# Weight tiles 512 bytes longer, with each unit's chunks at one of sixteen byte offsets, and a halved dynamic DMA scratch

## The chip, the cores and the metric

The kernel runs on one core of one Trainium2 chip. The metric is the device time of one execution in microseconds. A profiled execution gives the trace from which all rows below are taken.

## What is computed

Three layers of a transformer on 512 tokens (x) and 256 context tokens (ctx), width 2048, all in fp32. Cut to what matters for the weights:

```python
# layer 1, attention:  w_in is 2048 x 5120, w_out is 2048 x 2048
h = rmsnorm(x, pre_g) * (1 + scale) + shift ; hc = the same of ctx
proj = h @ w_in ; kv_c = hc @ w_in[:, 2048:3072]
y = concat(dense_attention, window_attention) * silu(z)
x = x + gate * rmsnorm(y @ w_out, post_g)
# layer 2, pooling: w_in is 2048 x 4096
proj = h @ w_in
y = (pooled(proj[:, :2048]) @ pool_w) * pool_scale * silu(proj[:, 2048:])
x = x + gate * rmsnorm(y @ w_out, post_g)
# layer 3: w_in is 2048 x 8192
proj = h @ w_in_2
y = concat(stick_breaking(q, k, v) * silu(z), group_norm(retention(q, k, v)) * silu(z))
x = x + gate * (y @ w_out_2)
# shift, scale, gate of each layer: silu(c) @ (2048 x 6144) + b
```

## The kernel before

**Chunks.** Every weight matrix is cut into units of 256 output columns (a few of 512, or of several column blocks side by side), and every unit into chunks of 512 KB: four slices of 128 rows by 256 columns, so 4 KB in each of the 128 partitions. There are 88 units and 376 chunks, numbered in one line through the three layers. Chunk i passes through four steps. SyncE loads it with one DMA into RAW[i % 5] (L1135) once TensorE is done with chunk i - 5. ScalarE rounds it to fp32r into the tile that `whi(i)` names (L1357, recorded at its helper L1272) once TensorE is done with chunk i - 4: WHI0, WHI1, WHI2 for i % 4 below 3, and WHITA for i % 4 = 3, or WHIY in the middle of layer 3. VectorE writes the rest, RAW - WHI, over RAW as WLO (L1751, recorded at L1634). TensorE then multiplies: each slice and each half of its columns takes three matmuls, the high part of the weights with the high and the low part of the activations (HHI, HLO) and the low part of the weights with HHI. That makes 4 x 2 x 3 = 24 matmuls of 512 columns a chunk.

**Roles.** All matmuls are recorded at the helper's line L2151 and all transposes at L2154. The trace names a matmul as out<-moving,stationary: `G<-HHI,WLO` streams 512 columns of HHI over a loaded 128 x 128 block of WLO. In `mm` and `mm2` stages the weights are the stationary operand. In `mt` (values of layer 1, 256 columns wide) and `mw` (values of layer 3, 512 columns wide) the weights are the moving operand: `G<-WLO,HHI`.

**Order.** The order on all engines is one list, written out by `make_plan`, which every engine's program walks. Side work (normalisation, rope, scores, softmax, the modulation vectors, whose weights stream through MWIDE) is put between the matmuls of the chunks.

**Places.** Tiles are laid out by hand in SBUF. The first free byte of a partition is 16,481, which rounds to 16,512, that is 128 above a multiple of 512. All large tiles up to MK are multiples of 512 bytes long, so HHI, HLO, RAW, WHI0 to WHI2, WHIY, MWIDE, SQ, TY and the like all start at 128 modulo 512. The small vectors behind them are not such multiples, so that the scratch region (base `s0`) starts at 384 modulo 512, and with it WHITA, PHI, PLO, QLO, KLO, PB, PT and XR. No tile that a matmul of 128 or more columns reads starts off a multiple of 64 bytes. HHI lies at 16,512, WHIY at 110,720, WHI0 at 135,296, WHITA at 224,128, PHI at 203,136 bytes.

```python
        tile, at = place(f"RAW{i}", [P, 4, 256], F32)
        WLO.append(place(f"WLO{i}", [P, 4, 256], F32R, at)[0])
    WHI3 = [place(f"WHI{i}", [P, 4, 256], F32R)[0] for i in range(3)]
...
                if i >= NR:
                    e.wait_ge(p_gemm, i - NR)
                e.o.dma_start(shaped(RAW[i % NR], chunks[i].shape[1]), chunks[i])
...
                cp(whi(i)[:, :, :], RAW[i % NR][:, :, :])
...
                tt(WLO[i % NR][:, :, :], RAW[i % NR][:, :, :], f(whi(i)[:, :, :]), SUB)
```

Of the kernel before, what the change touches and what calls it, by code (L numbers as in the profile page):

```python
# [5 lines left out]
F32 = mybir.dt.float32  # L6
F32R = mybir.dt.float32r
# [4 lines left out]
P = 128  # L12
D = 2048
KT = 16
SEQ = 512
# [64 lines left out]
def build(nc, ctx, T, out):  # L80
# [4 lines left out]
    top = [(base + 63) // 64 * 64]  # L85

    def place(name, shape, dt, at=None):
        size = 4
        for s in shape[1:]:
            size *= s  # L90
        if at is None:
            at = top[0]
            top[0] += (size + 31) // 32 * 32
            assert top[0] <= end - 32, (name, top[0], end)
        return nc.alloc_sbuf_tensor_at(name, list(shape), dt, offset=at), at

    HHI, h0 = place("HHI", [P, KT, SEQ], F32R)
    HLO, _ = place("HLO", [P, KT, SEQ], F32R)
    Y, y0 = place("Y", [P, KT, SEQ], F32)
    CT, _ = place("CT", [P, KT, CTX], F32, y0)  # L100
    CLO, _ = place("CLO", [P, KT, CTX], F32R, y0)
    CHI, _ = place("CHI", [P, KT, CTX], F32R, y0 + 4 * KT * CTX)
    XN = [place(f"XN{i}", [P, D], F32, h0 + 4 * i * D)[0] for i in range(6)]
    LATE = [place(f"LATE{i}", [P, 4, 256], F32, h0 + 4 * SEQ * (KT + 8 + 2 * i))[0] for i in range(4)]
    NR, NS = 5, 4
    RAW, WLO = [], []
    for i in range(NR):
        tile, at = place(f"RAW{i}", [P, 4, 256], F32)
        RAW.append(tile)
        WLO.append(place(f"WLO{i}", [P, 4, 256], F32R, at)[0])  # L110
    WHI3 = [place(f"WHI{i}", [P, 4, 256], F32R)[0] for i in range(3)]
    MRAW, MWIDE = [], []
    for i in range(2):
        tile, at = place(f"MRAW{i}", [P, 4, 256], F32)
        MRAW.append(tile)
        MWIDE.append(place(f"MWIDE{i}", [P, 2, 512], F32, at)[0])
    MACC, _ = place("MACC", [P, 512], F32)
    d0 = top[0]
    SQ2 = [place("SQ0", [P, SEQ], F32)[0]]
    tile, sq1 = place("SQ1", [P, SEQ], F32)  # L120
# [3 lines left out]
    QHI, _ = place("QHI", [P, SEQ], F32R, ty0)  # L124
    TT_, _ = place("TT", [P, SEQ], F32)
    DUMP, _ = place("DUMP", [P, D], F32, d0)
    RB, _ = place("RB", [P, 6, P], F32, d0 - 2048)
    IDN, _ = place("IDN", [P, P], F32)
    ONE, _ = place("ONE", [P, P], F32)
    CS, _ = place("CS", [P, SEQ], F32)  # L130
    SN, _ = place("SN", [P, SEQ], F32)
    MK, mk0 = place("MK", [P, 3, P], F32)
    COL, _ = place("COL", [P, 304], F32)
    MOD, _ = place("MOD", [P, 3, 48], F32)
    MODX, _ = place("MODX", [P, 32], F32)
    SC, _ = place("SC", [P, 48], F32)
    SM, _ = place("SM", [P, 48], F32)
    s0 = top[0]
    room = end - 32 - s0

    def scratch(name, shape, dt, off):
        size = 4
        for s in shape[1:]:
            size *= s
        assert off + size <= room, (name, off, size, room)
        return place(name, shape, dt, s0 + off)[0]

    K1 = 1024
# [26 lines left out]
    LSB = scratch("LSB", [P, SEQ], F32, 40 * K1)  # L175
    WB = [scratch(f"WB{i}", [P, SEQ], F32, 42 * K1 + i * 2 * K1) for i in range(2)]
    TA = [scratch(f"TA{i}", [P, SEQ], F32, 46 * K1 + i * 2 * K1) for i in range(2)]
    WHI_TA = scratch("WHITA", [P, 4, 256], F32R, 46 * K1)
    WHI_Y, _ = place("WHIY", [P, 4, 256], F32R, y0 + 4 * SEQ * 14)
    TRIR = scratch("TRIR", [P, P], F32R, 50 * K1)  # L180
    RESTR = scratch("RESTR", [P, P], F32R, 50 * K1 + 512)
    XO = [scratch(f"XO{i}", [P, SEQ], F32, 32 * K1 + i * 2 * K1) for i in range(4)]
    KLO = scratch("KLO", [P, 4, 768], F32R, 0)
    KHI = [place(f"KHI{i}", [P, 768], F32R, y0 + at)[0] for i, at in enumerate((16 * K1, 19 * K1, 24 * K1))]
# [4 lines left out]
    SQLO, _ = place("SQLO", [P, SEQ], F32R, sq1)  # L189
    SQHI, _ = place("SQHI", [P, SEQ], F32R, tm0)  # L190
    ONER, _ = place("ONER", [P, P], F32R, mk0)
# [18 lines left out]
    raw = [sig(f"raw{i}") for i in range(NR)]  # L210
# [8 lines left out]
    def on_chip(*names):  # L219
# [7 lines left out]
    a_intro, a_whi, a_xt, a_sq, a_rs, a_row, a_h, a_ev, a_exp, a_turn, a_silu, a_sqy = on_chip(  # L227
        "a_intro", "a_whi", "a_xt", "a_sq", "a_rs", "a_row", "a_h", "a_ev", "a_exp", "a_turn", "a_silu", "a_sqy")
    a_ph, a_st, a_out, a_sum = on_chip("a_ph", "a_st", "a_out", "a_sum")
    v_intro, v_wlo, v_xt, v_rs, v_xn, v_cols, v_h, v_acc, v_msum, v_mod, v_nr, v_sm, v_gate, v_silu = on_chip(  # L230
        "v_intro", "v_wlo", "v_xt", "v_rs", "v_xn", "v_cols", "v_h", "v_acc", "v_msum", "v_mod", "v_nr", "v_sm", "v_gate",
        "v_silu")
# [5 lines left out]
    MUL, ADD, SUB, MAX, MIN = ALU.mult, ALU.add, ALU.subtract, ALU.max, ALU.min  # L238

    def f(t):  # L240
        return t.bitcast(F32)
# [8 lines left out]
    def shaped(tile, nk):  # L250

        return tile[:, :, :].rearrange("p a n -> p (a n)").rearrange("p (t n) -> p t n", t=nk)
# [19 lines left out]
    units = [both(ev_w, 2048, 2304), weight(ev_w, 2560), weight(ev_w, 2816)]  # L272
# [28 lines left out]
    chunks = [c for u in units for c in u]  # L301
# [4 lines left out]
    stick0, stick1 = first_chunk[third + 1], first_chunk[third + 15] + 4  # L306
# [3 lines left out]
    last_y = max(i for i in fourths if i < stick1)  # L310
    next_ta = min(i for i in fourths if i >= stick1)

    def whi(i):

        if i % 4 < 3:
            return WHI3[i % 4]
        return WHI_Y if stick0 <= i < stick1 else WHI_TA

    nat = [("c", 0), ("c", 1)] + [("x", i) for i in range(4)]
    order0 = [nb for i in range(8) for nb in (i, 8 + i)]  # L320
# [794 lines left out]
    def sp_program(e):  # L1115
        e.o.dma_start(PR[:, :, :], T["small"].rearrange("a p n -> p a n")).then_inc(*par.up("par", by=16))
        e.o.dma_start(IDN[:, :], T["t_sq"][0]).then_inc(*cst.up("idn", by=16))
        e.o.dma_start(ONE[:, :], T["t_sq"][1]).then_inc(*cst.up("cst", by=16))
        for n in range(6):
            src = T["ctx"][0, n * P:(n + 1) * P, :] if n < 2 else T["x"][0, (n - 2) * P:(n - 1) * P, :]  # L1120
            e.o.dma_start(XN[n][:, :], src).then_inc(*xnd[n].up(n, by=16))
        for stage, *a in plan:
            if stage == "job_load":
                i, = a
                slot = job_slot[i]
                if job_before[i] is not None:
                    e.wait_ge(p_row, job_before[i])
                nb, c = jobs0[i]
                e.o.dma_start(rings[slot][:, :, :], weight(T["ev_mod_w"][0], 256 * nb)[c]).then_inc(  # L1129
                    *mraw[slot].up(("job", i), by=16))  # L1130
            elif stage == "load":
                i, = a
                if i >= NR:
                    e.wait_ge(p_gemm, i - NR)
                e.o.dma_start(shaped(RAW[i % NR], chunks[i].shape[1]), chunks[i]).then_inc(*raw[i % NR].up(i, by=16))  # L1135
            elif stage == "mod_load":
                n, = a
                if n >= 2:
                    e.wait_ge(v_acc, n - 2)
                else:  # L1140
                    e.wait_ge(p_row, last_in[n])
                w, nb, _, _, _ = mod_jobs[n // 8]
                e.o.dma_start(MWIDE[n % 2][:, :, :], wide(w, nb, n % 8)).then_inc(*mraw[n % 2].up(n, by=16))
            elif stage == "x_out":
                q, i = a
                if q == 3:
                    if i % 2:
                        e.wait_ge(v_out, (q, i))
                    else:
                        e.wait_ge(a_out, (q, i))  # L1150
                    e.o.dma_start(out[0, i * P:(i + 1) * P, 512 * q:512 * q + 512], XO[i][:, :]).then_inc(
                        *last[i].up((q, i), by=16))
        for i in range(4):
            e.wait_ge(last[i], (3, i))
# [108 lines left out]
    def act_program(e):  # L1263
# [7 lines left out]
        def cp(o, i, scale=1.0):  # L1271
            return e.o.activation(o, i, ACT.Copy, scale=scale)  # L1272
# [29 lines left out]
        for stage, *a in plan:  # L1302
            if stage == "x_sum":
                n, = a
# [21 lines left out]
            elif stage == "row_copy":  # L1326
                n, = a
# [17 lines left out]
            elif stage == "split":  # L1345
# [7 lines left out]
                elif i == next_ta:  # L1353
                    e.wait_ge(p_cum, (7, 0))
                    e.wait_ge(v_st, (7, 0, "ls"))
                    e.wait_ge(v_st, (7, 0, "lo"))
                cp(whi(i)[:, :, :], RAW[i % NR][:, :, :]).then_inc(*a_whi.up(i))  # L1357
            elif stage == "k_copy":
                side, nt, pair, u = a
                kh = 2 * side + nt  # L1360
# [268 lines left out]
    def dve_program(e):  # L1629
# [3 lines left out]
        def tt(o, a, b, op):  # L1633
            return e.o.tensor_tensor(o, a, b, op)  # L1634
# [43 lines left out]
        for stage, *a in plan:  # L1678
# [69 lines left out]
            elif stage == "split":  # L1748
                i, = a
                e.wait_ge(a_whi, i)  # L1750
                tt(WLO[i % NR][:, :, :], RAW[i % NR][:, :, :], f(whi(i)[:, :, :]), SUB).then_inc(*v_wlo.up(i))  # L1751
            elif stage == "mod_acc":
                t, c = a
                n = 8 * t + c
# [390 lines left out]
    def pe_program(e):  # L2145
# [35 lines left out]
        for stage, *a in plan:  # L2181
# [45 lines left out]
            elif stage == "kv":  # L2227
                k, what, part = a
                i = k // 4 * 2 + (0 if what == "k" else 1)
                wh, wl, j = whi(i), WLO[i % NR], k % 4  # L2230
                hi, lo = HHI[:, k, :], HLO[:, k, :]
                chi, clo = CHI[:, k, :], CLO[:, k, :]
                begin, end = k == 0, k == KT - 1
# [23 lines left out]
                    t.then_inc(*p_gemm.up(i, *([(0, 1 if what == "k" else "v")] if end else [])))  # L2257
            elif stage == "mm":
                kind, layer, u, i, c, nt, jj, pair, last = a
                wh, wl = whi(i), WLO[i % NR]  # L2260
                cols = slice(nt * P, nt * P + P)
                e.wait_ge(v_wlo, i)
                for j in (2 * jj, 2 * jj + 1):
# [16 lines left out]
                        t.then_inc(*p_gemm.up(*named))  # L2280
            elif stage == "mm2":
                kind, layer, u, i, uu, k0, nt, jj, pair = a
                wh, wl = whi(i), WLO[i % NR]
                cols = slice(nt * P, nt * P + P)
                e.wait_ge(v_wlo, i)
                for j in (2 * jj, 2 * jj + 1):
# [15 lines left out]
                                              *([(u, nt)] if k == 15 and uu == 2 else [])))  # L2302
            elif stage == "mt":
                layer, u, i, c, t_, pair, last, final = a
                wh, wl = whi(i), WLO[i % NR]
                bank = (G[pair] + [OB])[t_ // 2]
                o = bank[:, t_ % 2 * 256:t_ % 2 * 256 + 256]
                e.wait_ge(v_wlo, i)
# [18 lines left out]
                    t.then_inc(*p_gemm.up(i, *([(u, 1)] if last else [])))  # L2327
            elif stage == "mw":
                layer, u, i, c, t_, pair, last, final = a
                wh, wl = shaped(whi(i), 2), shaped(WLO[i % NR], 2)  # L2330
                o, cols = G[pair][t_ % 2][:, :], slice(t_ * P, t_ * P + P)
                e.wait_ge(v_wlo, i)
                for j in range(2):
# [300 lines left out]
```

## Time and profile before

| | us |
|---|---|
| median of 2 runs | 2536.39 (2535.85 to 2536.93) |
| the profiled execution's own time | 2535.82 |
| its span in the trace | 2534.0 |
| TensorE busy | 2497.7 (99%) |
| TensorE weight loads | 2020.2 (80%) |
| VectorE busy | 1623.8 (64%) |
| ScalarE busy | 973.6 (38%) |
| GpSimd busy | 110.7 (4%) |

The profiled execution took 1.8 us more than its span and 0.6 us less than the median of the runs. The granted TensorE clock was 0.995 over the span. A matmul's record runs until its last result is out (some 389 ns for 512 columns), and the next one begins before that; what counts for throughput is the distance between starts, which the chain of work shows as length over count.

### The profile page before, as it was taken

To read this page: it belongs to the slowest core of one execution; us is meant where nothing else is said; L and a number is where in the kernel's file an instruction comes from. 1 tells how busy PE (TensorE), PEld (TensorE's weight loads), DVE (VectorE), ACT (ScalarE), POOL (GpSimd) and SP (SyncE) were. 2 spreads that over 40 slices of the span, in tenths; PEclk is the share of its full clock that TensorE was granted. 3 is DMA by queue.
4 is the path that set the end of the run, shared out by engine and by line. 5 is a ranking of instruction groups with operands and counts; after the bars stand their busy time and mean duration, and the time that the engine had idled before them with its cause. 6 is when DMAs were issued, how large, how long until landed. Compare 5 with 4: busy or idle time off the path is not lost.

```text
span 2534.0 us, 30108 instructions
## 1 busy us (share of the span) xinstructions
PE 2497.7 (99%) x11975; PEld 2020.2 (80%) x11975; DVE 1623.8 (64%) x2444; ACT 973.6 (38%) x1549; POOL 110.7 (4%) x117
## 2 busy tenths in 40 slices
PE   7999999999999999999999999999999999999999
PEld 4789777777777887888888887888888787887887
DVE  4456776677776768776776768456365577656532
ACT  4232444444444333432434333445455432333421
POOL 0000000000000114000000113000000000000000
PEclk8999999999999999999999999999999999999999
DMA  9955433434433754666645754323222245532342
GB/s 350 336 193 185 127 110 121 125 125 133 132 101 136 258 180 157 208 200 211 200 162 175 249 175 158 111 76 91 80 87 84 75 151 169 175 112 89 123 154 83
DMA packets 293133, 390.58 MB, mean 154 GB/s; under 512 B 11698, under 2 KB 221234, under 8 KB 289154
## 3 DMA queue, kind: packets, MB, share of 16 engines
q1 hardware_dynamic: 287184, 355.84, 43.5%
q0 software_dynamic: 5808, 32.84, 3.5%
q8 instruction: 94, 1.54, 0.2%
q14 instruction: 45, 0.37, 0.1%
q10 hardware_dynamic: 2, 0.00, 0.0%
HBM read 371.85 MB, written 16.78 MB: 153 GB/s over the span
## 4 chain that ended last, share of the span: by engine, by line
PE 89%; DVE 5%; DMA 2%; ACT 2%; issue 1%; SPq 1%; POOL 0%; DVEq 0%; ACTq 0%; POOLq 0%
PE G L2151 74%; PE OB L2151 6%; PE S L2151 6%; PE TB L2154 2%; PE TB L2151 1%; DMA MRAW<-in_ev_mod_w 1%; DMA MORE<-in_ev_mod_w 1%; DVE WLO L1634 1%; DVE MACC L1640 1%; DVE TT L1634 1%; ACT PB L1445 1%; DVE SM L1862 0%; SPq L1129 0%; PE OB L2154 0%; DVE Y L1634 0%
## 5 line engine op out<-in xcount | busy, mean ns | idle before, releaser
L2151 PE MATMUL G<-HHI,WLO 128*128 128x512 f32 x2560 | 1001.0, 391 | 0.0
L2151 PE MATMUL G<-HHI,WHI 128*128 128x512 f32 x1964 | 801.8, 411 | 0.5 <-DVE CLO L1640 0.5
L2151 PE MATMUL G<-HLO,WHI 128*128 128x512 f32 x1928 | 753.2, 391 | 1.6 <-DVE HLO L1640 1.4
L2151 PEld LDWEIGHTS G<-HHI,WLO 128*128 128x128 f32 x2560 | 480.7, 188 | 104.3
L1272 ACT ACTIVATE WHI<-RAW 128x1024 fp32r<-128x1024 f32 x282 | 297.5, 1056 | 560.9 <-PE G L2151 501.6
L1634 DVE TENSOR_TENSOR WLO<-RAW,WHI 128x1024 fp32r<-128x1024 f32 x282 | 344.5, 1222 | 234.9 <-ACT WHI L1272 233.0
L2151 PEld LDWEIGHTS G<-HHI,WHI 128*128 128x128 f32 x1964 | 370.9, 189 | 80.3 <-issue 6.7
L2151 PEld LDWEIGHTS G<-HLO,WHI 128*128 128x128 f32 x1928 | 363.1, 188 | 79.7 <-issue 6.7
L1640 DVE SCALAR_TENSOR_TENSOR MACC<-MWIDE,SC,MACC 128x512 f32<-128x512 f32 x420 | 320.4, 763 | 39.2 <-DMA MWIDE<-in_w_ada 12.8
L2151 PE MATMUL G<-HHI,WHITA 128*128 128x512 f32 x536 | 215.0, 401 | 0.0
L2151 PE MATMUL G<-HLO,WHITA 128*128 128x512 f32 x536 | 209.2, 390 | 0.0
L1634 DVE TENSOR_TENSOR WLO<-RAW,WHITA 128x1024 fp32r<-128x1024 f32 x76 | 93.1, 1226 | 91.4 <-ACT WHITA L1272 91.4
L2151 PE MATMUL G<-WLO,HHI 128*128 128x512 f32 (+1 forms) x384 | 136.1, 354 | 0.0
L2151 PEld LDWEIGHTS G<-HLO,WHITA 128*128 128x128 f32 x536 | 100.9, 188 | 19.9 <-DVE HLO L1640 0.8
L2151 PEld LDWEIGHTS G<-HHI,WHITA 128*128 128x128 f32 x536 | 100.8, 188 | 19.9 <-issue 0.5
L2151 PE MATMUL G<-WHI,HHI 128*128 128x512 f32 (+1 forms) x272 | 103.6, 381 | 0.6 <-ACT K L1272 0.6
L1272 ACT ACTIVATE WHITA<-RAW 128x1024 fp32r<-128x1024 f32 x76 | 80.3, 1056 | 58.2 <-PE G L2151 52.6
L1269 ACT ACTIVATE SQ<-SQ 128x512 f32<-128x512 f32 x144 | 90.6, 629 | 25.4 <-DVE SQ L1640 22.4
L2151 PE MATMUL G<-WHI,HLO 128*128 128x512 f32 (+1 forms) x272 | 97.5, 358 | 0.0
L2151 PEld LDWEIGHTS G<-WLO,HHI 128*128 128x128 f32 x384 | 72.5, 189 | 10.3
L2151 PE MATMUL OB<-PT,VV 128*128 128x512 f32 (+2 forms) x192 | 74.7, 539 | 0.0
L1445 ACT ACTIVATE PB<-S,SM,COL 128x768 f32<-128x768 f32 x32 | 31.7, 992 | 103.5 <-DVE SM L1637 103.5
(347 smaller groups left out, 3060.7 us busy)
## 6 DMA issues: line engine op xcount, KB each, us to landing
RAW<-in_w_in SPq DMA_DIRECT2D x128, 512.0 KB, 3.7
MWIDE<-in_od_mod_w SPq DMA_DIRECT2D x96, 512.0 KB, 4.1
MWIDE<-in_w_ada SPq DMA_DIRECT2D x96, 512.0 KB, 4.6
RAW<-in_ev_w_in SPq DMA_DIRECT2D x80, 512.0 KB, 3.5
RAW<-in_od_w_in SPq DMA_DIRECT2D x64, 512.0 KB, 3.9
MWIDE<-in_ev_mod_w SPq DMA_DIRECT2D x32, 512.0 KB, 3.8
RAW<-in_ev_w_out SPq DMA_DIRECT2D x32, 512.0 KB, 3.3
RAW<-in_od_w_out SPq DMA_DIRECT2D x32, 512.0 KB, 3.3
```

Source lines behind the costliest of these rows:

```text
L1269: return e.o.activation(o, i, fn, bias=bias, scale=scale)
L1272: return e.o.activation(o, i, ACT.Copy, scale=scale)
L1445: e.o.activation(PB[n % 2][:, lo:768], S[:, lo:768], ACT.Exp, bias=nm, scale=1.0 if banded(h) else q_root_of(h, qt), accum_out=SM[:, i + 1 ...
L1634: return e.o.tensor_tensor(o, a, b, op)
L1640: return e.o.scalar_tensor_tensor(out=o, in0=a, scalar=s, in1=b, op0=op0, op1=op1)
L2151: return e.o.matmul(o, l, r, start=start, stop=stop, skip_group_check=True)
L2154: return e.o.transpose(o, i, IDN[:, :])
```

## The change

RAW, WLO, WHI0 to WHI2 and WHITA grow from 1024 to 1152 floats a partition. A new function `inside` picks 1024 of them, starting at float `FROM[unit % 16]`: byte offsets 0, 32, 64, 96, 128, 16, 48, 80, 112, 160, 192, 256, 320, 384, 448 and 8 for units 0 to 15, then again from 0. All chunks of a unit lie at the same offset in all their tiles. From `stick0` to `stick1` (chunks 228 to 299, layer 3) the offset is 0 in all tiles, and WHIY has no more room than before. To make room, the scratch for DMAs whose descriptors GpSimd writes is set to 8192 bytes, where it was 16,384; the first free byte of a partition goes from 16,481 to 8,289, and everything lies lower. `s0` is rounded so that the scratch region starts at 128 modulo 512 as all else does; TRIR and RESTR move up by 512 bytes.

Of the 376 chunks, 100 stay at offset 0. Offsets that are multiples of 64 bytes have 117 chunks (20, 17, 21, 13, 20, 16, 10 at 64, 128, 192, 256, 320, 384, 448), offsets 32, 96 and 160 have 24, 24 and 16, offsets 16, 48, 80 and 112 have 17, 20, 32 and 16, and offset 8 has 10. That is 276 chunks off zero, of which 159 are off a multiple of 64 bytes and 95 off a multiple of 32.

The instructions of all engines, their shapes, their waits and their order are the same before and after; only addresses differ.

```diff
@@ -105,10 +105,10 @@
     for i in range(NR):
-        tile, at = place(f"RAW{i}", [P, 4, 256], F32)
+        tile, at = place(f"RAW{i}", [P, 1152], F32)
         RAW.append(tile)
-        WLO.append(place(f"WLO{i}", [P, 4, 256], F32R, at)[0])
-    WHI3 = [place(f"WHI{i}", [P, 4, 256], F32R)[0] for i in range(3)]
+        WLO.append(place(f"WLO{i}", [P, 1152], F32R, at)[0])
+    WHI3 = [place(f"WHI{i}", [P, 1152], F32R)[0] for i in range(3)]
@@ -135,6 +135,7 @@
+    top[0] += (128 - top[0]) % 512
     s0 = top[0]
@@ -175,10 +176,10 @@
-    WHI_TA = scratch("WHITA", [P, 4, 256], F32R, 46 * K1)
-    WHI_Y, _ = place("WHIY", [P, 4, 256], F32R, y0 + 4 * SEQ * 14)
-    TRIR = scratch("TRIR", [P, P], F32R, 50 * K1)
-    RESTR = scratch("RESTR", [P, P], F32R, 50 * K1 + 512)
+    WHI_TA = scratch("WHITA", [P, 1152], F32R, 46 * K1)
+    WHI_Y, _ = place("WHIY", [P, 1024], F32R, y0 + 4 * SEQ * 14)
+    TRIR = scratch("TRIR", [P, P], F32R, 50 * K1 + 512)
+    RESTR = scratch("RESTR", [P, P], F32R, 51 * K1)
@@ -310,11 +311,25 @@
+    unit_of = [u for u, n in enumerate(units) for _ in n]
+    FROM = (0, 8, 16, 24, 32, 4, 12, 20, 28, 40, 48, 64, 80, 96, 112, 2)
+
+    def inside(slot, i):
+
+        at = 0 if stick0 <= i < stick1 else FROM[unit_of[i] % 16]
+        return slot[:, at:at + 1024].rearrange("p (a n) -> p a n", a=4)
+
     def whi(i):
 
         if i % 4 < 3:
-            return WHI3[i % 4]
-        return WHI_Y if stick0 <= i < stick1 else WHI_TA
+            return inside(WHI3[i % 4], i)
+        return inside(WHI_Y if stick0 <= i < stick1 else WHI_TA, i)
+
+    def raw_of(i):
+        return inside(RAW[i % NR], i)
+
+    def wlo(i):
+        return inside(WLO[i % NR], i)
@@ -1132,7 +1147,7 @@
-                e.o.dma_start(shaped(RAW[i % NR], chunks[i].shape[1]), chunks[i]).then_inc(*raw[i % NR].up(i, by=16))
+                e.o.dma_start(shaped(raw_of(i), chunks[i].shape[1]), chunks[i]).then_inc(*raw[i % NR].up(i, by=16))
@@ -1354,7 +1369,7 @@
-                cp(whi(i)[:, :, :], RAW[i % NR][:, :, :]).then_inc(*a_whi.up(i))
+                cp(whi(i)[:, :, :], raw_of(i)[:, :, :]).then_inc(*a_whi.up(i))
@@ -1748,7 +1763,7 @@
-                tt(WLO[i % NR][:, :, :], RAW[i % NR][:, :, :], f(whi(i)[:, :, :]), SUB).then_inc(*v_wlo.up(i))
+                tt(wlo(i)[:, :, :], raw_of(i)[:, :, :], f(whi(i)[:, :, :]), SUB).then_inc(*v_wlo.up(i))
@@ -2257,7 +2272,7 @@
-                wh, wl = whi(i), WLO[i % NR]
+                wh, wl = whi(i), wlo(i)
...
@@ -2614,7 +2629,7 @@
-    nc = bacc.Bacc("TRN2", target_bir_lowering=False, num_devices=1)
+    nc = bacc.Bacc("TRN2", target_bir_lowering=False, num_devices=1, dynamic_dma_scratch_size=8192)
```

## Rows read from the trace of the kernel before

**Rows 1.** The page, parts 1 and 2: busy us (share), instructions; busy tenths by slice

```profile
PE 2497.7 (99%) x11975; PEld 2020.2 (80%) x11975; DVE 1623.8 (64%) x2444; ACT 973.6 (38%) x1549; POOL 110.7 (4%) x117
...
PE   7999999999999999999999999999999999999999
```

**Rows 2.** The chain that ended last, in pieces: start us, us, what

```profile
1473.47 43.56 PE G L2151 x192
...
2199.50 38.08 PE G L2151 x168
...
1005.77 10.88 PE G L2151 x48
...
189.56 5.75 PE G L2151 x48
...
346.90 1.04 PE S L2151 x6
347.94 1.41 PE G L2151 x6
349.34 0.43 PE TB L2154 x4
349.78 1.38 PE G L2151 x6
```

**Rows 3.** Timeline of PE across a change from WHI2 to WHITA: start us, us, instruction

```profile
2209.31 0.39 PE L2151 MATMUL G<-WLO,HHI 128*128 128x512 f32 x1
2209.53 0.39 PE L2151 MATMUL G<-WHI,HHI 128*128 128x512 f32 x1
2209.76 0.39 PE L2151 MATMUL G<-WHI,HLO 128*128 128x512 f32 x1
2209.99 0.39 PE L2151 MATMUL G<-WLO,HHI 128*128 128x512 f32 x1
2210.22 0.39 PE L2151 MATMUL G<-WHITA,HHI 128*128 128x512 f32 x1
2210.44 0.39 PE L2151 MATMUL G<-WHITA,HLO 128*128 128x512 f32 x1
2210.67 0.39 PE L2151 MATMUL G<-WLO,HHI 128*128 128x512 f32 x1
2210.89 0.39 PE L2151 MATMUL G<-WHITA,HHI 128*128 128x512 f32 x1
```

**Rows 4.** Groups of PE by shape, 1475 to 1515 us: busy us, mean ns

```profile
L2151 PE MATMUL G<-HHI,WHI 128*128 128x512 f32 x42 | 16.3, 389 | 0.0
L2151 PE MATMUL G<-HHI,WHITA 128*128 128x512 f32 x18 | 7.0, 389 | 0.0
```

**Rows 5.** Weight loads, timeline and group: 256-column matmuls, then 1475 to 1515 us

```profile
471.37 0.28 PE L2151 MATMUL S<-KHI,QHI 128*128 128x256 f32 x1
471.49 0.28 PE L2151 MATMUL S<-KLO,QHI 128*128 128x256 f32 x1
471.60 0.51 PE L2151 MATMUL S<-KHI,QLO 128*128 128x512 f32 x2
...
L2151 PEld LDWEIGHTS G<-HHI,WLO 128*128 128x128 f32 x59 | 11.1, 188 | 2.3
```

**Rows 6.** Groups of the page, part 5: busy us, mean ns, idle before, releaser

```profile
L1272 ACT ACTIVATE WHI<-RAW 128x1024 fp32r<-128x1024 f32 x282 | 297.5, 1056 | 560.9 <-PE G L2151 501.6
L1634 DVE TENSOR_TENSOR WLO<-RAW,WHI 128x1024 fp32r<-128x1024 f32 x282 | 344.5, 1222 | 234.9 <-ACT WHI L1272 233.0
```

**Rows 7.** Timeline of SP, ACT and DVE around chunk work, and PE 16 us later

```profile
2206.47 0.47 SPq L1135 DMA_DIRECT2D RAW<-in_w_in  x1
...
2211.43 1.06 ACT L1272 ACTIVATE WHI<-RAW 128x1024 fp32r<-128x1024 f32 x1 [5.33 <-DMA RAW<-in_w_in]
...
2212.52 1.22 DVE L1634 TENSOR_TENSOR WLO<-RAW,WHI 128x1024 fp32r<-128x1024 f32 x1 [0.86 <-ACT WHI L1272]
...
2226.53 0.39 PE L2151 MATMUL G<-WHI,HHI 128*128 128x512 f32 x1
```

**Rows 8.** DMA issues: KB each, us to landing; then one stretch, PE to DMA share, GB/s

```profile
RAW<-in_od_w_in SPq DMA_DIRECT2D x64, 512.0 KB, 3.9
...
XR<-x_spill POOLq DMA_DIRECT2D x12, 1024.0 KB, 6.2
...
1386.70:1428.00 41.30, 41.30 (x184) 34.21 (x183) 32.07 (x40) 17.05 (x25) 8.06 (x7) 1.00 0.78 271
```

**Rows 9.** Groups of DVE by shape, 1017 to 1330 us: the pooling sums

```profile
L1634 DVE TENSOR_TENSOR UP<-UP,RC 128x512 f32<-128x512 f32 x16 | 10.0, 686 | 0.0
L1634 DVE TENSOR_TENSOR UP<-UP 128x2172 f32<-128x2172 f32 x4 | 9.7, 2413 | 0.0
L1634 DVE TENSOR_TENSOR UP<-UP,UP 128x2048 f32<-128x2048 f32 x4 | 9.1, 2285 | 0.0
```

**Rows 10.** Timeline of POOL: its DMA issues at the end of layer 1

```profile
963.92 0.58 POOL L1220 DMA_DIRECT2D x_spill<-Y  x1
...
975.09 0.58 POOL L1220 DMA_DIRECT2D x_spill<-Y  x1
```

More of the change, by code:

```diff
@@ L2229, in pe_program @@
                 i = k // 4 * 2 + (0 if what == "k" else 1)
-                wh, wl, j = whi(i), WLO[i % NR], k % 4
+                wh, wl, j = whi(i), wlo(i), k % 4
                 hi, lo = HHI[:, k, :], HLO[:, k, :]
@@ L2282, in pe_program @@
                 kind, layer, u, i, uu, k0, nt, jj, pair = a
-                wh, wl = whi(i), WLO[i % NR]
+                wh, wl = whi(i), wlo(i)
                 cols = slice(nt * P, nt * P + P)
@@ L2304, in pe_program @@
                 layer, u, i, c, t_, pair, last, final = a
-                wh, wl = whi(i), WLO[i % NR]
+                wh, wl = whi(i), wlo(i)
                 bank = (G[pair] + [OB])[t_ // 2]
@@ L2329, in pe_program @@
                 layer, u, i, c, t_, pair, last, final = a
-                wh, wl = shaped(whi(i), 2), shaped(WLO[i % NR], 2)
+                wh, wl = shaped(whi(i), 2), shaped(wlo(i), 2)
                 o, cols = G[pair][t_ % 2][:, :], slice(t_ * P, t_ * P + P)
```

## The prediction

> **What bounds the kernel now.** I read the page's busy shares first: TensorE is busy for 2497.7 of 2534.0 us [rows 1], so only 36 us are idle, and of the 40 slices the first alone, busy for seven tenths of its 63 us, holds 13 to 19 of them [rows 1]. Nothing that other engines do can bring more than that; what counts is how far apart the matmuls start. The chain of work shows it as length over count. In stretches with no side work between the matmuls it is 43.56 / 192 = 226.9 ns and 38.08 / 168 = 226.7 ns; 48 of 256 columns take 5.75 us, 119.8 ns each [rows 2]. The difference of the two widths, 106.9 ns for 256 columns, is 0.417 ns a column, which is the 2.4 GHz level at which the clock is granted there (1.00 [rows 8]). So 512 columns would take 213.3 ns, and each matmul has a fixed 13 ns on top, whether 256 or 512 columns follow. Each matmul also has a weight load of its own (11,975 of each [rows 1]). These 13 ns are the only thing in the trace on which the place of a weight tile could act with any weight. With side work between, six matmuls take 1.38 to 1.41 us, 230 to 235 ns each [rows 2], some 3 to 8 ns more.
>
> **The weight loads and the matmuls.** Does the gap depend on addresses? The trace of before holds a test, since WHITA and PHI start 256 bytes off HHI modulo 512 and WHI0 to WHI2 do not. Across the border from WHI2 to WHITA as moving operand the starts stay 0.22 to 0.23 us apart [rows 3]. With the weights stationary both groups have a mean of 389 ns a matmul [rows 4], within the stretch of 43.56 us at 226.9 ns. WHI0 to WHI2 lie near 135 KB, WHITA at 224 KB, so neither the high part of an address nor a shift by 256 bytes changes the gap. What no row shows is a shift that is no multiple of 256 bytes, since no such operand exists before. I bound its cost from both sides. Below: the gap goes away where the offset is not zero, 276 chunks x 24 matmuls x 13.3 ns = 88 us of gain. Above: the gap doubles there, 88 us of loss. I take zero, since the nearest rows (a shift of 256 bytes, three places in memory, both roles) show no difference at all.
>
> A longer weight load by itself has cover. Its record is 188 ns, but the loads of two 256-column matmuls follow each other at 0.12 and 0.11 us [rows 5], so one occupies its path for at most some 115 ns, and 512-column matmuls are 226.7 ns apart. A load that took twice as long at an odd offset would need 230 ns, 3 ns too many: 95 chunks off a multiple of 32 bytes x 24 x 3 ns = 7 us. Only a factor of three would show, 345 - 227 = 118 ns each. The stages where narrow matmuls have weights as stationary operand are the first unit, at offset 0, and the context part of unit 1, at 32.
>
> The Trainium skill has a rule here that speaks against a gain. The page "TensorE: Matmul & The Clock Gate", in Part 2, "What happens when you issue a matmul", says that TensorE has two independent read ports, and that loading the next weights takes no read bandwidth from the running matmul. By that rule the gap is no conflict of reads, and the sum is zero; by the opposite reading it is the 88 us. The equal gaps of [rows 3, 4] agree with the rule as far as they reach; they lower the chance that I give to the gain, but smaller shifts stay untested. The same page gives 215.7 ns as start to start of isolated warm matmuls of 512 columns; if the 226.7 ns fell to that in 276 chunks, an estimate is 276 x 24 x 11 ns = 73 us, inside the bound already set.
>
> **The split on ScalarE and VectorE.** Each chunk costs a copy of 1056 ns and a subtraction of 1222 ns [rows 6]. For VectorE the trace shows reads and writes off by 4 bytes and more: the pooling sums add UP to itself one to four floats further. The aligned shapes give (2285 - 686) / (2048 - 512) = 1.041 ns an element, so 2172 elements should take 2414 ns; they take 2413 [rows 9]. So the subtraction costs the same, and I take zero. For ScalarE no row shows it. I bound its copy by zero and by twice 1056 ns; both hide, because the copy has time. One chunk shows how much: its copy starts at 2211.43 and the low part is done at 2212.52 + 1.22 = 2213.74; TensorE begins this chunk (the third after the one that starts at 2210.22) at 2226.53 [rows 3, 7]. That is 12.8 us of slack. Over the kernel ScalarE waits 501.6 us for TensorE to free a WHI tile [rows 6]: it is TensorE that holds back the splits. Twice the copy is some 1.06 us of 12.8. If the cover were gone it would be 1.06 x 276 = 293 us.
>
> **The DMAs of the weights.** A load lands in 3.9 us or so [rows 8]; in the crowded stretch of [rows 7] it was issued at 2206.47 and the copy started at 2211.43, 5.0 us, with the same 12.8 us behind it. A landing would have to take over 17 us before TensorE waits. For lasting traffic the limit is the chunk period of 24 x 226.7 ns = 5.44 us: in the fullest stretch the 16 DMA engines are busy for 0.78 at 271 GB/s [rows 8]; of that a 512 KB chunk in 5.44 us is 96 GB/s, a share of 0.28, or 1.5 us of all engines a chunk. Up to a factor of (0.28 + 0.22) / 0.28 = 1.8 everything still fits, and up to 5.44 / 1.5 = 3.6 the weights alone do. I take no cost. What queues behind a late load on SyncE is the next MWIDE load, which has no TensorE work waiting but at the ends of layers.
>
> The Trainium skill has a rule that speaks against this change. Its page "DMA: Bandwidth & Descriptors", under "How a descriptor splits into AXI transactions", says that a descriptor which does not start at a multiple of 256 bytes pays for the unused bytes below its start, in beats of 32 bytes. If this held for the side that is written (the page speaks of reads), rows of 1 KB at 128 modulo 256 cost 36 beats before, offset 112 makes 40 of it, and offsets 128 and 384 make 32. That is an estimate of 11% more or less on a landing, 0.4 us of 3.9, beside 12.8 us of slack: the sum is zero by the rule and without it, only the landings of single units would tell. No run shows it yet.
>
> **The scratch and the shift of all tiles.** Everything lies 3.8 to 8.2 KB lower, and the scratch region at 128 in place of 384 modulo 512. By [rows 3, 4] this is nothing. Half the room for GpSimd's descriptors matters only when several of its DMAs are under way: at the end of layer 1 they are issued 11.2 us apart [rows 10], and the 1 MB ones land in some 6 us [rows 8]. Zero; were one of them held back by a whole landing, it is 6 us at three layer ends, 18 us at most.
>
> **The sum.** 0 + 0 + 0 + 0. The profiled execution took 2535.82 us, 0.6 us below the median of 2536.39; I predict the median unchanged, 2536. Its own width comes from the excess of 3 to 8 ns beside side work, which may come out otherwise at other addresses: 64 chunks of layer 1 and some 100 of layer 3 run so, 164 x 24 x 4 ns = 16 us either way, 2520 to 2552. A measurement of this kernel tells about 2% from no change, 51 us.
>
> **The rivals.** *The gap closes.* If the load of the next weights and the moving stream hit the same lines as long as both start alike modulo 64 bytes, a shift would remove the 13.3 ns: 2536 - 88 = 2448 with all 276 chunks, 2536 - 159 x 24 x 13.3 ns = 2485 with those off a multiple of 64. For it speaks that the gap is 13 ns at both widths, so once for each load. Against it speaks that 256 bytes change nothing, and that a gap for filling the array would look the same. Chance 0.07, of which 0.05 beyond 2%.
>
> *The gap widens (slower).* All operands start alike modulo 64 bytes now; if that is the favourable case, each shifted load or stream collides. The place is each of the 24 matmuls of a shifted chunk. The smallest price shown is the excess beside side work, 4.2 ns: 6624 x 4.2 ns = 28 us, 2564; the largest is a second gap, 2624. It passes 2% from 7.7 ns a matmul. For it: the excess of 3 to 8 ns shows that the stream can be disturbed. Against it: [rows 3, 4] again. Chance 0.09, of which 0.06 beyond 2%.
>
> *The loads land late (slower).* Writes off a multiple of 32 bytes cost more than 3.6 times as much; at 5 times a chunk takes 7.4 us in place of 5.44, 1.9 us x 95 = 181 us, 2717. Against it: rows of 1 KB have 31 whole pieces of 32 bytes at any offset. Chance 0.04, all beyond 2%.
>
> *It does not act.* A hundred chunks stay at offset 0, and the compiler or the chip may read in steps that make the offsets alike; that is my forecast with another reason.
>
> **How the numbers follow.** No change has 0.80, gap closes 0.07, gap widens 0.09, late loads 0.04. Faster by over 2% has 0.05, slower by over 2% 0.06 + 0.04 = 0.10, within 2% 0.85. No change fills 2520 to 2552; I widen this to 2510 and 2566, to take in slight forms of both gap cases, the 28 us of the smallest shown price above all.
>
> **What would show it.** The chain's undisturbed stretches in layer 2 and in the output products should stay at 226.7 ns a matmul for every unit, at 8 and 16 bytes as at 256. A closed gap would show as 213 to 220 ns in some units and not in others, a widened one as 235 or more; the stretch of layer 3 at offset 0 is the control in the same trace. The subtraction should stay at 1222 ns, the copy at 1056, the landings at 3.3 to 4 us. I am wrong if the spacing goes with the offset, or if TensorE starts to wait for WLO.

## The result: 24 us slower, all of it between the starts of matmuls

The kernel after takes 2560.36 us, median of 2 runs (2559.32 to 2561.40), against 2536.39 before: a ratio of 1.0091, 95% interval 1.0074 to 1.0108. That is 24.0 us more: under 2%, but the interval leaves no room for an equal time. The profiled execution has a span of 2559.6 us, 25.6 more than before. The page, parts 1 and 2, then the groups of part 5 and the issues of part 6 [rows 1, 6, 8]:

```profile
PE 2523.4 (99%) x11975; PEld 2020.2 (79%) x11975; DVE 1625.5 (64%) x2444; ACT 972.9 (38%) x1549; POOL 111.1 (4%) x117
...
PE   7999999999999999999999999999999999999999
...
L2166 PE MATMUL G<-HHI,WLO 128*128 128x512 f32 x2560 | 1007.8, 394 | 0.0
...
L1287 ACT ACTIVATE WHI<-RAW 128x1024 fp32r<-128x1024 f32 x282 | 297.3, 1055 | 576.0 <-PE G L2166 519.9
L1649 DVE TENSOR_TENSOR WLO<-RAW,WHI 128x1024 fp32r<-128x1024 f32 x282 | 344.5, 1222 | 248.7 <-ACT WHI L1287 246.1
...
RAW<-in_od_w_in SPq DMA_DIRECT2D x64, 512.0 KB, 3.8
```

TensorE's busy time rose by 25.7 us, as much as the span. The busy time of the weight loads (2020.2 us), the copy (1055 ns), the subtraction (1222 ns) and these landings (3.8 us) did not move, and ScalarE waits longer for TensorE, not the other way round. So TensorE does the same work more slowly. The chain shows where: the same pieces of layer 2, which took 43.56 us for 192 matmuls before [rows 2], each cover several units now. The second fence is of the same view, cut to stretches in which all weights lie at one offset: in order of time 256, 384, 448, 0, 80, 160, 32, 96 and 16.

```profile
1030.38 38.62 PE G L2166 x168
...
1108.81 44.19 PE G L2166 x192
...
1187.51 44.81 PE G L2166 x192
...
1445.49 44.83 PE G L2166 x192
```

```profile
1035.87 15.64 PE G L2166 x69
...
1074.80 22.31 PE G L2166 x96
...
1097.11 5.49 PE G L2166 x24
...
1114.05 16.32 PE G L2166 x72
...
1232.76 22.04 PE G L2166 x95
...
1277.64 22.64 PE G L2166 x97
...
1411.22 22.63 PE G L2166 x97
...
1456.46 22.71 PE G L2166 x97
...
1501.71 22.40 PE G L2166 x96
```

Length over count: offsets 0 and 256 give 226.7 ns; 448 gives 228.8, 80 gives 232.0, 384 gives 232.4, 16 and 32 give 233.3, 160 gives 233.4 and 96 gives 234.1. The clock has no part in it. A row of the windows view for the stretch at offset 32, ending in granted clock, DMA share and GB/s:

```profile
1411.30:1433.70 22.40, 22.40 (x98) 18.04 (x97) 19.15 (x24) 8.56 (x12) 3.91 (x4) 1.00 0.68 238
```

The granted clock is 1.00, the 2.4 GHz level, as it was before [rows 8]. A single-tile view of the unit at offset 32 tells what got longer:

```profile
L2166 PE MATMUL G<-HHI,WLO x4: 395/396/397, 1411.1 to 1413.2; 128*128 128x512 f32 x4
L2166 PEld LDWEIGHTS G<-HHI,WLO x3: 187/188/188, 1411.5 to 1412.9; 128*128 128x128 f32 x3
```

The record of the weight load is 188 ns as before, so the load of the moved weights did not itself become longer. That of the matmul, which streams the unmoved HHI, is 396 in place of 389. The profile models where a matmul ends, so these 7 ns are no second proof beside the distance between starts.

Summed over the two traces, start to start, unit by unit: units off zero +23.7 us, chunks 228 to 299 (at offset 0) 0.0 us, unit 0, where TensorE waits for the first loads, +3.4, all other matmuls -1.7. The 3.4 us of unit 0 are no effect of an offset: the kernel below with all offsets at zero shows 4.3 us there and takes as long as the kernel before. Layer 3 at offset 0 is the control, shown by one piece of the chain before and the same piece after:

```profile
2031.99 28.61 PE G L2151 x126
```

```profile
2051.70 28.61 PE G L2166 x126
```

One of the four executions of the kernel below with its activations moved by 160 bytes, the profiled one, was disturbed (3115.74 us at a granted clock of 0.75); its time is left out, and the readings come from a second trace.

### The profile page after: what moved, and what is told of

It reads as the page before. It is cut to its first block, busy times and chain, and to the rows that moved or that the text cites. A ratio compares the mean times of both kernels' runs of the same rounds, so it can differ in the third digit from the quotient of the medians.

```text
span 2559.6 us, 30108 instructions
## 1 busy us (share of the span) xinstructions
PE 2523.4 (99%) x11975; PEld 2020.2 (79%) x11975; DVE 1625.5 (64%) x2444; ACT 972.9 (38%) x1549; POOL 111.1 (4%) x117
## 4 chain that ended last, share of the span: by engine, by line
PE 90%; DVE 4%; DMA 2%; ACT 2%; issue 1%; SPq 1%; POOL 0%; DVEq 0%; ACTq 0%; POOLq 0%
PE G L2166 75%; PE OB L2166 6%; PE S L2166 6%; PE TB L2169 2%; PE TB L2166 1%; DMA MRAW<-in_ev_mod_w 1%; DMA MORE<-in_ev_mod_w 1%; DVE MACC L1655 1%; DVE WLO L1649 1%; DVE TT L1649 1%; ACT PB L1460 0%; DVE SM L1877 0%; SPq L1144 0%; PE OB L2169 0%; DMA LATE<-in_ev_mod_w 0%
## 5 line engine op out<-in xcount | busy, mean ns | idle before, releaser
L1287 ACT ACTIVATE WHI<-RAW 128x1024 fp32r<-128x1024 f32 x282 | 297.3, 1055 | 576.0 <-PE G L2166 519.9
L1649 DVE TENSOR_TENSOR WLO<-RAW,WHI 128x1024 fp32r<-128x1024 f32 x282 | 344.5, 1222 | 248.7 <-ACT WHI L1287 246.1
```

## The experiments

Eleven kernels in twelve runs, in the order of the questions. All are edits of the changed kernel, and each was compared with the kernel before on the same chip (2536.4 to 2537.5 us). Distances are those of 512-column matmuls without side work between, in ns from start to start; offsets are taken modulo 256 bytes.

**Is it the offsets at all?** One kernel keeps the longer tiles, the lower places and the halved scratch, but takes every offset back to zero. The other also moves every tile of the kernel up by 64 bytes.

```diff
-    FROM = (0, 8, 16, 24, 32, 4, 12, 20, 28, 40, 48, 64, 80, 96, 112, 2)
+    FROM = (0,) * 16
```

> All chunks at offset 0; tile lengths, scratch size and the place of the scratch region as in the changed kernel. Theory R (the distance between matmul starts depends on where the weights lie relative to the activations, modulo 256 bytes): undisturbed stretches back at 226.7 ns, time 2536, within 3 us of the kernel before. Theory S (the halved scratch or the shift of all tiles costs something): 2545 to 2560.

```diff
-    top = [(base + 63) // 64 * 64]
+    top = [(base + 63) // 64 * 64 + 64]
...
-    top[0] += (128 - top[0]) % 512
+    top[0] += (192 - top[0]) % 512
...
+    FROM = (0,) * 16
```

> As e1_zero, and every tile, weights and activations alike, 64 bytes higher, so all start at 192 modulo 256. Theory R (relative place): 226.7 ns in undisturbed stretches, 2536. Rival A (absolute place: a weight tile is read fast only where it starts at 128 modulo 256, and at 192 it costs the 233.3 ns that the units at offsets 64 and 320 show): 233 ns everywhere, 2575 to 2590.

The first took 2537.69 us, ratio 1.0002 (0.9993 to 1.0012), the second 2537.54, 1.0002 (0.9992 to 1.0011). The chain of the second kernel:

```profile
1102.71 43.56 PE G L2166 x192
```

226.9 ns, to the digit that of [rows 2]. The scratch, the lengths and the shift cost nothing, and neither does the one other absolute place tried. What is left is how weights and activations lie to each other; the next two kernels test it.

**Is it the distance between the two operands?** One kernel leaves all weights at zero and moves HHI and HLO up by 160 bytes. Another leaves the activations and puts every chunk of the kernel at 96, all but the high parts in WHIY, which has no room for it. Modulo 256 the weights then lie 96 above the activations in both.

```diff
+    top[0] += 160
     HHI, h0 = place("HHI", [P, KT, SEQ], F32R)
     HLO, _ = place("HLO", [P, KT, SEQ], F32R)
+    top[0] += (128 - top[0]) % 512
...
+    FROM = (0,) * 16
```

> As e1_zero, with HHI and HLO (and what shares their place) 160 bytes higher and the weights at offset 0, so that the weights lie 96 bytes above the activations modulo 256. Theory R: the 234 ns of the units at offset 96 in all stretches with HHI and HLO, while the pool products, whose activations are PHI and PLO, stay at 226.7 ns; time 2575 to 2590. Rival A (absolute place of the weights): 226.7 ns and 2536.

```diff
-        at = 0 if stick0 <= i < stick1 else FROM[unit_of[i] % 16]
+        at = 24
...
-        return inside(WHI_Y if stick0 <= i < stick1 else WHI_TA, i)
+        if stick0 <= i < stick1:
+            return WHI_Y[:, :].rearrange("p (a n) -> p a n", a=4)
+        return inside(WHI_TA, i)
```

> All chunks of all layers at offset 96 (WHIY stays, for want of room). Theory R: the same distance modulo 256 as in e3_act160, reached from the other side, so the same time but for the 8 chunks of the pool products and 18 splits of WHIY: within 5 us of 2583. If instead the landing, rounding or subtraction of displaced weights costs something of its own, this kernel is slower than e3_act160 by more than 5 us.

Activations moved: 2582.77 us, 1.0177 (1.0160 to 1.0194). The same kernel once more, for its trace, took 2581.61 us:

> The kernel of e3_act160 once more, for its trace. Theory R: undisturbed stretches with HHI and HLO at 234 ns as the units at offset 96 in the changed kernel; the pool products, with PHI and PLO, at 226.7 ns. Rival A (absolute place): all at 226.7 ns.

Weights moved: 2582.47 us, 1.0181 (1.0166 to 1.0196). The chain of the first, then of the second kernel:

```profile
1033.02 39.35 PE G L2168 x168
```

```profile
1035.80 39.35 PE G L2167 x168
...
1115.38 44.97 PE G L2167 x192
```

Both give 39.35 / 168 = 234.2 ns: moving the one operand down or the other up is the same thing, and the cost reaches 45 to 46 us when all but a few high parts have it. The kernel with the moved activations has a control inside. Its pooling products stream PHI and PLO, which did not move. Groups of TensorE from 1098 to 1130 us, busy us and mean ns of one:

```profile
L2168 PE MATMUL G<-HHI,WLO 128*128 128x512 f32 x30 | 11.9, 396 | 0.0
...
L2168 PE MATMUL G<-PHI,WLO 128*128 128x512 f32 x16 | 6.2, 389 | 0.0
...
L2168 PE MATMUL G<-HHI,WHITA 128*128 128x512 f32 x12 | 4.8, 397 | 0.0
```

```profile
1100.91 10.20 PE G L2168 x45
```

Same weight tiles, same stretch: 389 ns with PHI, 396 with HHI; the chain, cut to the matmuls with PHI and PLO, gives 10.20 us for 45 matmuls, 226.7 ns. With all chunks at 96 the copy still takes 1055 ns, the subtraction 1222, and the landings of `in_od_w_in` 3.9 us as in [rows 8]: at 96, where DMA, ScalarE and VectorE find the tiles costs nothing.

**Must all weights be displaced?** Here only the high parts are, at 96; RAW and WLO are at zero.

```diff
-        at = 0 if stick0 <= i < stick1 else FROM[unit_of[i] % 16]
+        at = 0 if stick0 <= i < stick1 else more
...
-            return inside(WHI3[i % 4], i)
-        return inside(WHI_Y if stick0 <= i < stick1 else WHI_TA, i)
+            return inside(WHI3[i % 4], i, 24)
+        return inside(WHI_Y if stick0 <= i < stick1 else WHI_TA, i, 24)
```

> As e1_zero, with the high parts (WHI0 to WHI2, WHITA) of all chunks 96 bytes up outside chunks 228 to 299, and RAW and WLO at offset 0. Two of three weight loads are then displaced. Theory R: the excess over 226.7 ns is about two thirds of the 7.5 ns at offset 96, some 231.5 ns, 2555 to 2570. If only the writes of ScalarE or the DMA landings at odd places were the cause, RAW at 0 takes it away: 2536.

2553.39 us, 1.0064 (1.0049 to 1.0079), 1.6 us below what was expected. Its chain:

```profile
1028.11 38.65 PE G L2166 x168
...
1067.20 38.83 PE G L2166 x168
```

230.1 and 231.1 ns: two of three loads displaced cost 3.4 to 4.4 of the 7.5 ns, and there are two patterns though every unit is laid out alike. It is not one fixed price per load, which would be two thirds, 5.0 ns.

**Which offsets, and why two patterns?** Two kernels carry other tables, so that one trace reads out sixteen values, and one has all chunks at 16 (again without WHIY), an offset that had shown 226.7 in unit 21 of the changed kernel and 233.3 in others.

```diff
+    FROM = (0, 62, 63, 60, 56, 58, 52, 44, 36, 6, 3, 1, 10, 18, 26, 30)
```

> The changed kernel with sixteen other byte offsets: 0, 248, 252, 240, 224, 232, 208, 176, 144, 24, 12, 4, 40, 72, 104, 120. Theory R (relative place modulo 256 decides): offsets just below 256 act like small negative shifts, so none is faster than 226.7 ns and most lie at 229 to 234 ns; time 2550 to 2570. Rival M (the first sixteen offsets missed a better place): some unit runs below 226 ns in undisturbed stretches.

```diff
+    FROM = (30, 29, 31, 34, 94, 33, 38, 42, 46, 47, 49, 50, 54, 55, 59, 22)
```

> The changed kernel with a third list of byte offsets: 120, 116, 124, 136, 376, 132, 152, 168, 184, 188, 196, 200, 216, 220, 236, 88. Theory R: no unit below 226.7 ns in undisturbed stretches, 376 (120 + 256) behaves as 120, the rest mostly at 228 to 234 ns; 2545 to 2560. Rival M: a unit below 226 ns shows that the gap itself can be made shorter by the place.

```diff
-        at = 0 if stick0 <= i < stick1 else FROM[unit_of[i] % 16]
+        at = 4
```

> All chunks at offset 16. In the changed kernel unit 53 at this offset runs at 233.3 ns, but three chunks of unit 21 run at 226.7 ns after a break. Theory L (two repeating patterns exist at this offset, and the break before a stretch picks one): stretches at 226.7 and at 233.3 ns side by side, time 2545 to 2575. Theory O (the offset alone sets the distance; unit 21 is an accident of neighbouring units at other offsets): all at 233.3 ns, 2575 to 2585.

The tables took 2558.15 us, 1.0083 (1.0068 to 1.0098), and 2560.53, 1.0093 (1.0075 to 1.0112), the latter 0.5 us above the upper end of what was expected. Distances with stationary weights, worked out from the starts of all matmuls of the units without side work in the three traces, from the tenth matmul behind a break on:

| ns | offsets in bytes |
|---|---|
| 226.7 | 0, 120, 132; at times 16, 240, 252 |
| 228 to 230.2 | 24, 116, 176, 192; at times 12, 240 |
| 230.7 to 232.4 | 4, 8, 80, 128, 152, 184, 200, 208, 216, 232, 236; at times 124 |
| 233 to 234.3 | 12, 16, 32, 40, 48, 64, 72, 88, 96, 104, 112, 124, 136, 144, 160, 168, 188, 196, 220, 224, 248; at times 128, 208, 252 |

Adding 256 changes nothing (0 and 256, 64 and 320, 128 and 384, 120 and 376 and, to 0.4 ns, 192 and 448). There is no rule by powers of two: 128 is slow, 120 and 132 are fast, 124 and 136 are slow. Three stretches of the chain of the last kernel, at 124, 120 and 132, give 233.3, 226.7 and 226.6 ns:

```profile
1157.28 20.53 PE G L2166 x88
...
1371.35 30.83 PE G L2166 x136
...
1502.74 21.53 PE G L2166 x95
```

None of the 41 offsets tried, of the 64 that there are in steps of 4 bytes, goes below 226.6 to 226.7 ns. The kernel with all chunks at 16 took 2562.35 us, 1.0100 (1.0083 to 1.0117), and its chain alternates:

```profile
1028.52 38.10 PE G L2167 x168
...
1067.06 39.20 PE G L2167 x168
```

226.8 and 233.3 ns, at one offset, one clock and the same tiles. Between the pieces lie four transposes; what differs is how matmuls resume behind them. Single distances form short repeating groups (226 and 227 at offset 0; 231, 232 and 235 at 32), and a group, once entered, is kept to the next break. At offset 0 it takes six to eleven matmuls behind a break until 226 and 227 stand, at 120 at most four. That made 120 a candidate for the stretches with side work, where every few matmuls there is a break.

**Can an offset beat zero?** All chunks at 120; then with the chunks whose weights are the moving operand at 136, the mirror image of 120; then with those at 0.

```diff
-        at = 0 if stick0 <= i < stick1 else FROM[unit_of[i] % 16]
+        at = 30
...
     Y, y0 = place("Y", [P, KT, SEQ], F32)
+    top[0] += 512
...
-    WHI_Y, _ = place("WHIY", [P, 1024], F32R, y0 + 4 * SEQ * 14)
+    WHI_Y, _ = place("WHIY", [P, 1152], F32R, y0 + 4 * SEQ * 14)
```

With this room WHIY moves too, here and in the two kernels that follow.

> All chunks of all layers at offset 120, WHIY too (512 bytes of room behind Y). In e5_other the one unit type seen at 120 in an undisturbed stretch ran at 226.7 ns, and after a break the distance settled after 3 matmuls (235, 238, 230, then 226 and 227) where offset 0 takes 9 (235, 234, 236, 224, 231, 235, 229, 232, 231). Theory R with settling: 22 ns less after each of some 300 breaks, 5 to 9 us below the kernel before, 2528 to 2532. Rival: 120 holds only for the few chunks seen, the other role of the weights (moving, in the values of layer 3) or other chunks fall into a slow pattern: 2540 to 2575.

```diff
+        moving = i < 8 and i % 2 or unit_of[i] == 2 or chunks[i].shape[1] == 2
+        at = 34 if moving else 30
```

> Weights at offset 120 where they are the stationary operand, and at 136 (that is -120 modulo 256) where they are the moving operand (the value chunks of layer 1 and the wide units of layer 3). Theory P (what counts is the place of the stationary operand minus that of the moving one): the wide units, at 234 to 237 ns in e9_all120, return to 226.7 to 228 ns, and the 4.4 us that the other units gained there remain, so 2531 to 2533. Rival Q (the difference has no sign, or 136 is slow in itself as it is for stationary weights in e10_more, 233.3 ns): the wide units at 233 ns, 2536 to 2540.

```diff
+        moving = i < 8 and i % 2 or unit_of[i] == 2 or chunks[i].shape[1] == 2
+        at = 0 if moving else 30
```

> As e11_roles with the moving weights at offset 0. Both theories: the wide units as before, 226.7 to 229.5 ns, the gain of 4.4 us elsewhere remains; 2531 to 2534. Under theory P e11_roles is faster than this one by up to 1 us, since the wide units with side work settle sooner.

All at 120 took 2538.96 us, 1.0010 (1.0001 to 1.0019), not the gain expected, and just under the 2540 to 2575 of its rival. Units with stationary weights came out 4.4 us shorter in sum, but the four wide units of layer 3, whose weights are the moving operand, 6.0 us longer (234 to 240 ns; the longest piece is in the second of them).

```profile
1813.02 23.03 PE G L2166 x96
```

With those at 136 the time was 2537.26, 0.9999 (0.9990 to 1.0008): the wide units were 4.2 us longer, and the theory that only the signed difference of the operands counts fell for this pair; its rival, with 2536 to 2540, came true. The other units kept only 2.9 of the 4.4 us, for a reason that was not looked for. With those at 0 it was 2533.33 us, 0.9983 (0.9974 to 0.9992), 3.6 us under the kernel before on the same chip and the fastest of all. Of some 4.6 us that the units with stationary weights gained in its trace, 3.9 lie in layers 1 and 3, where side work makes the breaks. The chain in one chunk of the first wide unit, at 120, at 136 and at 0:

```profile
1611.97 5.86 PE G L2166 x25
```

```profile
1613.11 5.60 PE G L2167 x24
```

```profile
1611.26 5.44 PE G L2167 x24
```

234.4, 233.3 and 226.7 ns. The kernel before has the same there:

```profile
1613.50 5.44 PE G L2151 x24
```

## Why the prediction was wrong

**The bound was read rightly.** TensorE was busy for 99% before and is after; the place of a weight tile could act only through the distance between starts, and did so only there.

**The step that failed is "I take zero, since the nearest rows (a shift of 256 bytes, three places in memory, both roles) show no difference at all"**, in the part on weight loads and matmuls. The rows were right and the inference was not. A shift of 256 bytes costs nothing because the effect repeats every 256 bytes (226.7 ns at 0 and 256, 233.3 at 64 and 320), and the places in memory were all equal modulo 256 to the activations. The rows of before sampled one phase of a periodic thing several times; they bore on no other phase, and could not carry 0.80 of the chance.

**The rival that came true was the widened gap**, given 0.09. Its smallest price, 4.2 ns for each of 6624 matmuls, made 28 us and 2564; measured are 23.7 us in those units, 3.6 ns each, and 2560.36. That the 4.2 ns came so near is luck: they were taken from side work, which is another thing, and [rows 2] show 3.3 to 8.3 ns there, not 4.2. The time also lies within 2510 to 2566 only because the range was widened for this rival; the forecast's own 2520 to 2552 missed it. The sign named for a widened gap, 235 ns or more, was set too high: the stretches came out at 228 to 234.3. The rival's premise, that equal starts are the favourable case, holds in steady stretches against all offsets tried but 120 and 132, which equal it, and 16, 240 and 252, which do at times. The average hides two sizes: 5 to 7.5 ns for most offsets in layer 2 and the output products, and on average some 1.5 ns in units 3 to 18 of layer 1 and 2.2 in layer 3, where side work had already lifted the distance to 230 to 235 ns [rows 2]. Units 3 to 18 of layer 1 have together 2.1 us more, as much as three or four undisturbed units. So the excess beside side work and the cost of an offset do not add.

**The bounds.** Gain and loss of up to 88 us (13.3 ns a matmul) were taken from both sides. The loss reaches 7.5 ns in full, 45 to 46 us with the weights 96 above the activations. The gain never came: the 13.3 ns at zero offset survive all 41 displacements tried, so they are no collision that one of these removes. The rival of the closed gap fell.

**"It does not act"** was the forecast with another reason, and fell with it: a step of 4 bytes, from 120 to 124, is worth up to 6.6 ns.

**Loads.** A longer load of the weights, costed at 7 us where it took twice as long, did not occur: its record is 188 to 189 ns in all of these traces. The distance between the matmuls grew over loads of the same length.

**Right at zero** were VectorE (1222 ns), ScalarE (1055), the landings (3.5 to 3.8 us by tensor, against 3.3 to 3.9; those of `in_od_w_out` went from 3.3 to 3.6, but are at 3.5 with all offsets at zero too, so that is not the offset), and the scratch, the lengths and the shift, together 1.0002 with the offsets taken back. The width of 16 us "either way" for side work at other addresses was not needed: with offsets zero at the new addresses the time is the same to 0.1%.

**The two rules of the Trainium skill.** The displaced tiles lengthen the distance between matmuls and not the load's record, and only by their place relative to what streams. "TensorE: Matmul & The Clock Gate", Part 2, "What happens when you issue a matmul", says that two independent read ports keep the next weights' load from taking bandwidth from the running matmul. The runs fit this only with a limit: by it the kernels with the offset and without would tie, and they are 46 us apart with all chunks at 96. The page "DMA: Bandwidth & Descriptors", "How a descriptor splits into AXI transactions", gave an estimate of up to 11% on landings. Counted the same way, offset 96 makes an estimate of 8%, 0.3 us of 3.9. With all chunks at 96 the landings of `in_od_w_in` take 3.9 us, as before and as with all at zero; no run here shows that effect on the side that is written.

**What stays open.** That load and stream disturb each other is inferred, from the dependence on their relative place and from two of three displaced loads costing about half; no run took the loads away from the matmuls. The signed difference explains the moving role at 64 and 96 (weights moving at 64 give 228.9 ns as stationary weights at 192 do; at 96, 233.3 as at 160) but not at 16 (231.7), 120 (234 to 240) and 136 (233.3, where 226.7 should stand). Perhaps the stream's own start counts there too; that is only argued. Which event in a break picks one of two patterns was not found.

## What to carry to other kernels

In a kernel bound by TensorE with a weight load for every matmul, let stationary and moving operands start alike modulo 256 bytes and treat any other offset as something to measure: padding a tile by something other than a multiple of 256 bytes can cost 3% of the matmul time, and no view shows it as a wait: it is seen in length over count. A row that shows "no difference" for one step of an address is no evidence for smaller steps; ask which phases of a possible period it sampled. A table that gives each unit a value of its own, with a stretch left at zero as control, reads sixteen values from one trace; but look at each value in more than one stretch, since one offset can run in two patterns.

## What the runs showed that was not expected

- The distance between matmul starts depends on the relative place of the operands modulo 256 bytes: 226.7 to 234.3 ns for 512 columns at the 2.4 GHz level, and 234 to 240 with moving weights at 120.
- Fine structure down to 4 bytes: 226.7 at 120, about 233 at 124 in most units, 226.7 at 132, 233.3 at 136.
- One layout can run in two patterns, 226.8 and 233.3 ns at offset 16, chosen at a break in the stream; what in the break chooses was not found.
- An offset of 120 matches 0 in steady stretches and recovers faster behind a break: together with moving weights at 0 it makes 2533.33 us, ratio 0.9983.
